# Three of eight experts in plain fp32 on 64 columns, two array halves, alternating with the others

## The chip, the cores and the metric

The kernel runs on one core of one Trainium2 chip. The metric is the device time of one execution in microseconds (us), the median of three runs. The five engines have queues of their own and meet at semaphores: TensorE (PE in the profile), VectorE (DVE), ScalarE (ACT), GpSimd (POOL) and SyncE (SP, which here issues the weight loads).

## The reference

A trunk of two layers on 256 tokens of width 1024, all in float32: retention and a dense SwiGLU in the first, a state-space mixer (S5) and a mixture of experts in the second, each behind a root-mean-square norm and added to the residual, and a last norm. What the change touches is the mixture: eight experts with a hidden width of 3584, of which each token uses two.

```python
logits = xf @ router
top_logits, top_idx = lax.top_k(logits, 2)
gates = softmax(top_logits)
# for each expert e, on the tokens that chose it:
y = (silu(x @ w_gate[e]) * (x @ w_up[e])) @ w_down[e]
# each token: the sum of its two experts' rows, times their gates
```

256 tokens with two choices are 512 rows, 64 an expert on average. Each expert has 44 MB of weights, 352 MB in all.

## The kernel before, in words

**Units.** All weights stream through SBUF in units of 1 MB, 128 partitions by 2048 numbers. SP loads unit n (L549 to L571) into one of six raw slots, and may do so when DVE has split the unit that held the slot (the wait at L569; the profile has the load itself at L570). ACT copies it, rounded, into one of three slots `weights_hi` (L892 to L901), as soon as it has landed and TensorE is done with the unit three before. DVE writes the rest, raw minus hi, into `weights_lo` (L1267 to L1271). TensorE then makes each product from three (L1751 to L1755): hi x hi, hi x lo, lo x hi, each at the rate of the rounded type. A unit is 12 matmuls of 128 stationary columns (the tokens) on 512 moving columns (the weights).

**Experts.** An expert has 42 units in 21 blocks of two (L1934 to L1968, `ffn`). The hidden width is cut in seven steps of 512, and the order is gate 0, up 0, then for s = 1 to 6 gate s, up s, down s-1, and down 6 at the end. ACT takes silu of the gate bank, DVE multiplies by the up bank (`act_rows`), TensorE transposes the four tiles of that (`turn`), and ACT and DVE split it, for the down units to use. ACT and DVE have this work written out between their splits, by the unit's number in the expert (L962 to L985, L1351 to L1378), and do it in that order. All eight experts use 128 slots of rows, in the order of their numbers. A second pass follows only if an expert has over 128 tokens; with these inputs it is skipped.

**Rows.** DVE picks the first expert's rows with a product against a pick matrix. POOL works out each row's slot in a chain of small operations, writes the normed rows to a table in HBM with four indirect DMAs (L841), then works out where they come back from. SP loads an expert's 128 rows of that table into `slot_rows` (L587) and TensorE turns them (L2252) ahead of the expert's last down block; SP also writes the result rows out (L591). The last expert's result doesn't go by HBM but by a product. POOL fetches the other rows back (L860) during the last expert.

Of the kernel before, what the change touches and what calls it, by code (L numbers as in the profile page):

```python
# [14 lines left out]
F32 = mybir.dt.float32  # L15
# [50 lines left out]
SPARE_U0 = MOE_U0 + RAW + AHEAD  # L66

# [99 lines left out]
def trunk(nc, A, consts, out):  # L167
    with ExitStack() as ctx:
# [84 lines left out]
        put_g = place("put_gated", [TT, P], F32, K_OFF + 26624)  # L253
        final_gain = place("final_gain_row", [D], F32, H_OFF + 16384)
# [9 lines left out]
        def small(name, shape, dt=F32):  # L264
            size = -(-4 * math.prod(shape) // 32) * 32
            small_at[0] += size
            assert small_at[0] <= H_OFF
            return place(name, shape, dt, small_at[0] - size)

# [37 lines left out]
        key = small("slot_key", [TT, EXPERTS])  # L307
        r_second = small("is_in_second_pass", [TT, EXPERTS])
# [47 lines left out]
        unused_set = sem("unused_set")  # L356
# [11 lines left out]
        warm_ready = sem("warm_rows_ready")  # L368
# [75 lines left out]
        counted = sem("tokens_counted")  # L444
# [95 lines left out]
        def _(sp):  # L540
# [8 lines left out]
            def load(n, kt, src, e=None):  # L549
# [5 lines left out]
                else:  # L555
                    signal = landed[ring_number(n, e) % RAW]
                    if n >= RAW:
# [11 lines left out]
                        sp.wait_ge(lo_ready, count(last + 1, e, FFN_UNITS))  # L569
# [11 lines left out]
            for p in range(2):  # L581
                sp.dma_start(from_slots[p][0:1, :], zeros[0:1, :]).then_inc((y_sent, nothing_landed)[p], 16)

            def slot_range(p, e):
                return bass.ds(e * SLOTS + (1 + ROWS * p), SLOTS)

            def load_slots(p, e):  # L587
                sp.wait_ge(gathered, count(EXPERTS * p, e, 1))
                sp.dma_start(slot_rows[:, :], to_slots[slot_range(p, e), :]).then_inc(slots_landed, 16)

            def send_y(p, e):  # L591
                sp.wait_ge(y0_copied, count(EXPERTS * p + 1, e, 1))
                sp.wait_ge(y1_copied, count(EXPERTS * p + 1, e, 1))
                sp.dma_start(from_slots[p][slot_range(0, e), :], y_rows[:, :]).then_inc(y_sent, 16)

            def experts(p):
                u0 = MOE_U0 + p * EXPERTS * FFN_UNITS
                if p:
                    load_slots(p, 0)

                def expert(e, first, last):
                    for i, (kt, src) in enumerate(ffn_sources(
                            A["moe_w_gate"][0, e], A["moe_w_up"][0, e], A["moe_w_down"][0, e])):
                        if i == 10 and not first:
                            send_y(p, e - 1)
                        if i == 24 and not last:
                            if first and not p:
                                sp.wait_ge(rows_sent, 16 * 2 * TT)
                            load_slots(p, e + 1)
                        load(u0 + i, kt, src, e)  # L610

                expert(0, True, False)
                with sp.Fori(1, LAST) as e:
                    expert(e, False, False)
                expert(LAST, False, True)

            experts(0)
            sp.wait_ge(keys_done, 1)
            flag = sp.value_load(over[0:1, 0:1], min_val=0, max_val=1)
            with sp.If(flag > 0):  # L620
                experts(1)
                send_y(1, LAST)
# [7 lines left out]
        def _(pool):  # L630
# [195 lines left out]
            tt(choice[1][:, :, :], chosen[:, :, :], choice[0][:, :, :], ALU.subtract)  # L826
            pool.wait_ge(pick_ready, 1)
            ts(r_second[:, :, :], key[:, :, :], float(SLOTS), None, ALU.is_gt, ALU.bypass)
            tt(r_cum[:, :, :], key[:, :, :], first_row, ALU.add)
            ts(row_of[0][:, :, :], r_second[:, :, :], float(ROWS - SLOTS), None, ALU.mult, ALU.bypass)  # L830
            tt(r_cum[:, :, :], r_cum[:, :, :], row_of[0][:, :, :], ALU.add)
# [6 lines left out]
            pool.wait_ge(nothing_landed, 16 * (2 * EXPERTS + 1))  # L838
            for t in range(TT):
                for j in range(2):  # L840
                    pool.indirect_dma_start(to_slots, bass.IndirectOffsetOnAxis(ap=pair_i[:, 0, j, t:t + 1], axis=0),  # L841
                                            hn[:, t, :], None).then_inc(rows_sent, 16)
            tt(row_of[1][:, :, :], r_cum[:, :, :], r_second[:, :, :], ALU.mult)
            tt(row_of[0][:, :, :], r_cum[:, :, :], row_of[1][:, :, :], ALU.subtract)
            link(nc.gpsimd.memset(row_of[0][:, :, LAST:EXPERTS], 0.0))
# [5 lines left out]
            both_choices(share[:, :, :], gate_w[:, :, :])  # L851
            nc.gpsimd.tensor_copy(pair_i[:, 1:3, :, :], pair[:, 1:3, :, :]).then_inc(shares_ready, 1)
# [11 lines left out]
            pool.wait_ge(y_sent, 16 + 16 * LAST)  # L864
# [3 lines left out]
            with pool.If(flag > 0):  # L868
                pool.wait_ge(y_sent, 16 + 16 * (LAST + EXPERTS))
                pool.wait_ge(scatter_added, 1)  # L870
                rows_come_back(1)
# [3 lines left out]
        def _(act):  # L875
# [16 lines left out]
            def split_hi(n, e=None):  # L892
# [6 lines left out]
                if n >= SPLIT:  # L899
                    act.wait_ge(used, count(n - SPLIT + 1, e, FFN_UNITS))  # L900
                copy(w_hi[:, n % SPLIT, :], raw_unit(n, e)).then_inc(hi_ready, 1)  # L901

            def norm_rows():

                act.wait_ge(unused_set, 1)
# [56 lines left out]
            def ffn(u0, s0, tts, e=None, each=None):  # L962

                silu_at = {ffn_first(s) + 4: s for s in range(STEPS)}
                evac_at = {7 if s == 0 else 41 if s == STEPS - 1 else 6 * s + 6: s for s in range(STEPS)}
                for i in range(FFN_UNITS):
                    if i in silu_at:
                        s = s0 + silu_at[i]

                        act.wait_ge(used, count(u0 + ffn_first(silu_at[i]) + 2, e, FFN_UNITS))  # L970
                        if s:
                            act.wait_ge(mult_done, count(s, e, STEPS))
                        nc.scalar.activation(gated[:, 0:tts, :], PS[:, 0:tts, :], ACT.Silu).then_inc(silu_done, 1)
                    if i in evac_at:
                        s = s0 + evac_at[i]
                        act.wait_ge(act_t_done, count(s + 1 - STEPS, e, STEPS))
                        copy(ht_hi[evac_at[i] % 2][:, 0:tts, :, :],
                             PS[:, tts:2 * tts, :].rearrange("p t (f c) -> p t f c", f=FT)).then_inc(act_hi, 1)
                    if each:
                        each(i)  # L980
                    if i < AHEAD:
                        continue
                    split_hi(u0 + i, e)

# [201 lines left out]

            def gather_hi(g):
# [4 lines left out]
            def y_out(p, e):  # L1192
                act.wait_ge(used, count(MOE_U0 + (p * EXPERTS + 1) * FFN_UNITS, e, FFN_UNITS))
                if not (isinstance(e, int) and e == 0 and p == 0):
                    act.wait_ge(y_sent, count(16 + 16 * (EXPERTS - 1) * p, e, 16))
                copy(y_rows[:, 0:512], PS[:, 4, :]).then_inc(y0_copied, 1)

            def last_y_out():

                act.wait_ge(first_half_done, 1)  # L1200
                act.wait_ge(y_sent, 16 + 16 * LAST)
                copy(y_rows[:, 0:512], PS[:, 4, :]).then_inc(y0_copied, 1)

            def experts(p):
                u0 = MOE_U0 + p * EXPERTS * FFN_UNITS
                if p:
                    gather_hi(EXPERTS * p + 1)
                    for i in range(AHEAD):
                        split_hi(u0 + i)

                def expert(e, first, last):
                    def each(i):
                        if i == 2 and not first:
                            y_out(p, e - 1)
                        if i == 19 and last and p == 0:
                            act.wait_ge(put_t_done, 1)
                            copy(put_g[:, :, :], PS[:, 6, 0:2 * P].rearrange("p (a b) -> p a b", a=2)).then_inc(put_ready, 1)
                    ffn(u0, STEPS * (1 + EXPERTS * p), 1, e, each)
                    if not last:
                        gather_hi(count(EXPERTS * p + 2, e, 1))  # L1220
                        for i in range(AHEAD):
                            split_hi(u0 + FFN_UNITS + i, e)
# [6 lines left out]
            experts(0)  # L1229
            act.wait_ge(keys_done, 1)  # L1230
            flag = act.value_load(over[0:1, 0:1], min_val=0, max_val=1)
            with act.If(flag > 0):
                last_y_out()
                experts(1)
                y_out(1, LAST)
# [19 lines left out]
        def _(dve):  # L1255
# [11 lines left out]
            def split_lo(n, e=None):  # L1267

                dve.wait_ge(hi_ready, count(n + 1, e, FFN_UNITS))
                tt(w_lo[:, n % SPLIT, :], raw_unit(n, e), w_hi[:, n % SPLIT, :].bitcast(F32),  # L1270
# [80 lines left out]
            def ffn(u0, s0, tts, e=None, each=None):  # L1351
                mult_at = {ffn_first(s) + 6: s for s in range(STEPS)}
                evac_at = {7 if s == 0 else 41 if s == STEPS - 1 else 6 * s + 6: s for s in range(STEPS)}
                for i in range(FFN_UNITS):
                    if i in mult_at:
                        s = s0 + mult_at[i]
                        dve.wait_ge(silu_done, count(s + 1, e, STEPS))

                        dve.wait_ge(used, count(u0 + ffn_first(mult_at[i]) + 4, e, FFN_UNITS))
# [980 lines left out]
```

## Time and profile before

| what | value |
|---|---|
| median of three runs | 1580.86 us (1580.41 to 1581.86) |
| span of the profiled execution | 1580.7 us, 23580 instructions |
| PE, PEld busy | 1565.6, 1306.7 us |
| DVE, ACT, POOL busy | 1213.7, 982.1, 271.8 us |
| HBM read, written | 461.23 MB, 15.21 MB, 301 GB/s over the span |

Busy times are of one profiled execution, whose own time is its span. A matmul's record is longer than its share of the engine's time, because matmuls overlap; the distance between the starts of two of them is what one costs. PEld is the load of stationary columns, beside the matmuls. A wait is put down to what ended it. The DMA share counts the time of packets, and can pass 1.

### The profile page before, as it was taken

To read this page: it belongs to the slowest core of one execution; us is meant where nothing else is said; L and a number is where in the kernel's file an instruction comes from. 1 tells how busy PE (TensorE), PEld (TensorE's weight loads), DVE (VectorE), ACT (ScalarE), POOL (GpSimd) and SP (SyncE) were. 2 spreads that over 40 slices of the span, in tenths; PEclk is the share of its full clock that TensorE was granted. 3 is DMA by queue.
4 is the path that set the end of the run, shared out by engine and by line. 5 is a ranking of instruction groups with operands and counts; after the bars stand their busy time and mean duration, and the time that the engine had idled before them with its cause. 6 is when DMAs were issued, how large, how long until landed. Compare 5 with 4: busy or idle time off the path is not lost.

```text
span 1580.7 us, 23580 instructions
## 1 busy us (share of the span) xinstructions
PE 1565.6 (99%) x9466; PEld 1306.7 (83%) x9466; DVE 1213.7 (77%) x825; ACT 982.1 (62%) x732; POOL 271.8 (17%) x244
## 2 busy tenths in 40 slices
PE   9999999999999999999999999999999999999997
PEld 8788889999988888888888888888888888888885
DVE  5556566555558658888888888888888888888897
ACT  5443454333454347777777777777777777777775
POOL 5599316200037008100000000000000000000100
PEclk9999999999999999999999999999999999999999
DMA  9544657865511368999999999999999999999993
GB/s 350 171 159 156 205 161 274 298 200 185 186 38 57 115 247 316 394 392 371 381 362 366 383 367 361 388 364 363 384 371 352 387 371 352 387 374 347 398 392 147
DMA packets 202143, 469.18 MB, mean 297 GB/s; under 512 B 7784, under 2 KB 20288, under 8 KB 202064
## 3 DMA queue, kind: packets, MB, share of 16 engines
q1 hardware_dynamic: 199872, 461.13, 80.7%
q0 software_dynamic: 2048, 6.88, 1.5%
q8 instruction: 55, 0.90, 0.2%
q14 instruction: 24, 0.20, 0.0%
q10 hardware_dynamic: 144, 0.07, 0.0%
HBM read 461.23 MB, written 15.21 MB: 301 GB/s over the span
## 4 chain that ended last, share of the span: by engine, by line
PE 93%; DVE 3%; ACT 2%; POOL 1%; issue 1%; DMA 0%; ACTq 0%; DVEq 0%; POOLq 0%
PE PS L1746 90%; PE PS L1875 2%; DVE weights_lo L1265 1%; ACT weights_hi L884 1%; POOL b_padded L784 1%; PE PS L2096 0%; ACT c_padded L884 0%; PE PS L2255 0%; DVE residual L1265 0%; POOL param_tmp L643 0%; DMA constants<-in_constants 0%; DVE act_rows L1265 0%; PE PS L1845 0%; ACT x_transposed_hi L934 0%; DVE act_rows L1416 0%
## 5 line engine op out<-in xcount | busy, mean ns | idle before, releaser
L1265 DVE TENSOR_TENSOR weights_lo<-weights_raw,weights_hi 128x2048 fp32r<-128x2048 f32 (+1 forms) x419 | 963.0, 2307 | 254.5 <-ACT weights_hi L884 252.9
L884 ACT ACTIVATE weights_hi<-weights_raw 128x2048 fp32r<-128x2048 f32 (+1 forms) x419 | 800.9, 1913 | 364.1 <-PE PS L1746 354.9
L1746 PE MATMUL PS<-weights_hi,gathered_hi 128*128 128x512 f32 x896 | 355.1, 396 | 0.3 <-DVE gathered_lo L1627 0.3
L1746 PE MATMUL PS<-weights_hi,gathered_lo 128*128 128x512 f32 x896 | 355.1, 396 | 0.0
L1746 PE MATMUL PS<-weights_lo,gathered_hi 128*128 128x512 f32 x896 | 352.3, 393 | 0.0
L1746 PE MATMUL PS<-weights_hi,act_transposed_hi 128*128 128x512 f32 x624 | 252.8, 405 | 0.0
L1746 PE MATMUL PS<-weights_hi,act_transposed_lo 128*128 128x512 f32 x624 | 247.1, 396 | 0.0
L1746 PE MATMUL PS<-weights_lo,act_transposed_hi 128*128 128x512 f32 x624 | 245.8, 394 | 0.0
L1746 PEld LDWEIGHTS PS<-weights_hi,gathered_lo 128*128 128x128 f32 x896 | 168.2, 188 | 41.2
L1746 PEld LDWEIGHTS PS<-weights_lo,gathered_hi 128*128 128x128 f32 x896 | 168.2, 188 | 41.1
L1746 PEld LDWEIGHTS PS<-weights_hi,gathered_hi 128*128 128x128 f32 x896 | 168.2, 188 | 40.0 <-DVE gathered_lo L1627 0.4
L1746 PE MATMUL PS<-x_transposed_hi,weights_hi 128*128 128x256 f32 x640 | 181.2, 283 | 1.3 <-DVE weights_lo L1265 1.1
L1746 PE MATMUL PS<-x_transposed_lo,weights_hi 128*128 128x256 f32 x640 | 179.7, 281 | 0.0
L1746 PE MATMUL PS<-x_transposed_hi,weights_lo 128*128 128x256 f32 x640 | 179.7, 281 | 0.0
L860 POOL DMA_INDIRECT row_back<-results_by_slot,pair_index x4 | 7.4, 1861 | 824.8 <-DMA results_by_slot<-expert_rows 823.9
L1746 PEld LDWEIGHTS PS<-weights_hi,act_transposed_lo 128*128 128x128 f32 x624 | 117.1, 188 | 28.6
L1746 PEld LDWEIGHTS PS<-weights_lo,act_transposed_hi 128*128 128x128 f32 x624 | 117.4, 188 | 26.5 <-issue 0.7
L1746 PEld LDWEIGHTS PS<-weights_hi,act_transposed_hi 128*128 128x128 f32 x624 | 117.3, 188 | 25.7 <-issue 0.7
L1746 PEld LDWEIGHTS PS<-x_transposed_hi,weights_hi 128*128 128x128 f32 x640 | 120.7, 189 | 2.6 <-DVE weights_lo L1265 1.3
L1746 PEld LDWEIGHTS PS<-x_transposed_lo,weights_hi 128*128 128x128 f32 x640 | 120.7, 189 | 0.3
L1746 PEld LDWEIGHTS PS<-x_transposed_hi,weights_lo 128*128 128x128 f32 x640 | 120.7, 189 | 0.0
L1746 PE MATMUL PS<-weights_hi,x_transposed_hi 128*128 128x512 f32 x192 | 76.2, 397 | 0.1
(283 smaller groups left out, 1273.4 us busy)
## 6 DMA issues: line engine op xcount, KB each, us to landing
weights_raw<-in_moe_w_up SPq DMA_DIRECT2D x111, 1024.0 KB, 6.8
weights_raw<-in_moe_w_down SPq DMA_DIRECT2D x111, 1024.0 KB, 6.6
weights_raw<-in_moe_w_gate SPq DMA_DIRECT2D x110, 1024.0 KB, 6.8
weights_raw<-in_ret_w_in SPq DMA_DIRECT2D x24, 1024.0 KB, 6.6
weights_raw<-in_ffn_w_gate SPq DMA_DIRECT2D x14, 1024.0 KB, 5.2
weights_raw<-in_ffn_w_up SPq DMA_DIRECT2D x14, 1024.0 KB, 5.1
weights_raw<-in_ffn_w_down SPq DMA_DIRECT2D x14, 1024.0 KB, 4.9
weights_raw<-in_ret_w_out SPq DMA_DIRECT2D x8, 1024.0 KB, 4.9
```

Source lines behind the costliest of these rows:

```text
L784: nc.gpsimd.tensor_scalar(b_pad[:, i0:i1, :, :, c].rearrange("p i j m n -> p (i j) m n"), rows.rearrange("p i j m n -> p (i j) m n"), cst[ ...
L860: pool.indirect_dma_start(back[t][j][:, :], None, from_slots[p], bass.IndirectOffsetOnAxis(ap=pair_i[:, 1 + p, j, t:t + 1], axis=0)).then_ ...
L884: return nc.scalar.activation(o, i, ACT.Copy)
L1265: return nc.vector.tensor_tensor(o, a, b, op)
L1746: return nc.tensor.matmul(o, l, r, start=start, stop=stop)
L1875: ins = nc.tensor.transpose(PS[:, bank, ft * P:(ft + 1) * P], act_rows[:, t, ft * P:(ft + 1) * P], ident)
```

## The change

The eight experts are put in a new order at run time. Expert 0 stays first. POOL sorts the others by their count of tokens, and ranks 1, 2 and 3, the three with the fewest, are the light ones; ranks 4 to 7 follow. SP reads each expert's number from SBUF and loads by it. The light ones have room for 64 rows each (an excess goes to the second pass). With the inputs used, experts 0 to 7 get 59, 61, 70, 66, 70, 59, 72 and 55 rows by the reference, so the light ones have 55, 59 and 61. Their units aren't split: TensorE reads the raw slot as the moving operand of plain fp32 products, with the 64 tokens as the stationary columns of one half of the array. In gate and up units one half takes the first 256 columns of the weights and the other half the last; in down units each half takes 512 of the 1024. So an unsplit unit's raw slot comes free when TensorE has used the unit. Split units have a count of their own for the `weights_hi` slots.

The order of units is: expert 0 whole; two blocks of rank 4; then a block of the heavy ranks and one of the light in turn, 63 times; then the last 19 blocks of rank 7. ACT's and DVE's small work for a light block stands at the second heavy unit two heavy blocks on. Slots are loaded and results sent by POOL, two halves of 512 columns for a light result, and the gathered rows are turned and copied in two halves through one bank in place of two.

Core of the diff:

```diff
+FIRST, LIGHT, HEAVY = 0, (1, 2, 3), (4, 5, 6, 7)
+BLOCKS = [("gate", 0), ("up", 0), *((kind, s - (kind == "down")) for s in range(1, STEPS) for kind in ("gate", "up", "down")),
+          ("down", STEPS - 1)]
+LAG = 2
+def small_after(k):
+    j = k - LAG
+    return j if 0 <= j < len(LIGHT) * len(BLOCKS) else None
+def units_in_order():
+    order = [(FIRST, i) for i in range(FFN_UNITS)]
+    for k in range(len(HEAVY) * len(BLOCKS)):
+        for ranks, at in ((HEAVY, k), (LIGHT, small_after(k))):
+            if at is not None:
+                q, b = block_of(ranks, at)
+                order += [(q, 2 * b), (q, 2 * b + 1)]
+    return order
...
@@ SP, load @@
-                        sp.wait_ge(lo_ready, count(last + 1, e, FFN_UNITS))
+                        if is_whole(last):
+                            sp.wait_ge(lo_ready, count(splits(last), e, FFN_UNITS))
+                        else:
+                            sp.wait_ge(used, last + 1)
...
@@ SP, order of the loads @@
+                for m, (q, i) in enumerate(ORDER):
+                    if q not in expert:
+                        if len(expert) == 1:
+                            sp.wait_ge(shares_ready, 1)
+                        expert[q] = sp.value_load(expert_at_i[0:1, q:q + 1], min_val=1, max_val=EXPERTS - 1)
...
@@ POOL, ahead of the rows' numbers (12 operations), more behind the scatters @@
+            pool.wait_ge(count_ready, 1)
+            ts(sort_key[:, :], token_count[:, :], float(EXPERTS * SLOTS), None, ALU.mult, ALU.bypass)
+            tt(sort_key[:, :], sort_key[:, :], expert_row, ALU.add)
...
+            tt(table[:, :, :], inner(sort_key[:, :]), outer(sort_key[:, :]), ALU.subtract)
+            ts(table[:, :, :], table[:, :, :], 0.0, None, ALU.is_lt, ALU.bypass)
+            over_table(rank[:, :])
...
@@ ACT, split_hi @@
-                    act.wait_ge(used, count(n - SPLIT + 1, e, FFN_UNITS))
+                    act.wait_ge(used, count(SPLIT_UNITS[SPLIT_NUMBER[n] - SPLIT] + 1, e, FFN_UNITS))
...
@@ DVE, behind split_lo(MOE_U0 + 2) @@
+            nc.vector.tensor_copy(token_count[:, :], PS[:, 6, 64:64 + EXPERTS]).then_inc(count_ready, 1)
...
@@ DVE, small work @@
+            def after_small(j):
+                q, b = block_of(LIGHT, j)
+                kind, s = BLOCKS[b]
+                if kind == "up":
+                    done = STEPS * (q - LIGHT[0]) + s
+                    dve.wait_ge(silu_small, done + 1)
+                    dve.wait_ge(used, NUMBER[q, 2 * b + 1] + 1)
+                    if done:
+                        dve.wait_ge(turned_small, done)
+                    tt(act_small[:, :], gated_small[:, :], PS[:, 2, 0:HALF_FC], ALU.mult).then_inc(mult_small, 1)
...
@@ DVE (and ACT likewise), for unit i of the heavy rank number at @@
+                        if at:
+                            l = FFN_UNITS * (at - 1) + i
+                            j = small_after((l - 5) // 2) if l % 2 else None
+                            if j is not None:
+                                after_small(j)
+                        if at or i >= AHEAD:
+                            split_lo(number(i))
...
@@ PE, a light block @@
+                def turn(s):
+                    pe.wait_ge(mult_small, STEPS * (q - LIGHT[0]) + s + 1)
+                    for i in range(2):
+                        ins = nc.tensor.transpose(PS[:, 2, i * P:(i + 1) * P], act_small[:, i * P:(i + 1) * P], ident)
+                    ins.then_inc(turned_small, 1)
+                if kind == "down":
+                    if s < STEPS - 1:
+                        turn(s + 1)
...
+                                ins = mm(PS[tile[dh], 7, :], act_t_small[s % 2][:, ft, :], w[:, k, dh * 512:dh * 512 + 512],
+                                         s == 0 and ft == 0, s == STEPS - 1 and ft == FT - 1)
...
+                if kind == "gate":
+                    if s == 1:
+                        turn(0)
...
+                        for h in range(2):
+                            ins = mm(PS[tile[h], bank, 0:HALF_FC], x_small[:, kt, :], w[:, k, h * HALF_FC:(h + 1) * HALF_FC],
+                                     kt == 0, kt == KT - 1)
```

## Rows read from the trace of the kernel before

**Rows 1.** The page: busy us of the engines; granted clock in 40 slices.

```profile
PE 1565.6 (99%) x9466; PEld 1306.7 (83%) x9466; DVE 1213.7 (77%) x825; ACT 982.1 (62%) x732; POOL 271.8 (17%) x244
...
PEclk9999999999999999999999999999999999999999
```

**Rows 2.** Who waited for whom, 640 to 1580 us: us in total, times, longest.

```profile
ACT weights_hi L884 <- PE PS L1746: 172.3, 233, 1.2
...
SPq L570 <- DVE weights_lo L1265: 727.8, 314, 3.7
```

**Rows 3.** Gathered rows' tile (count, ns, starts); the chain from 560 us.

```profile
L1746 PEld LDWEIGHTS PS<-weights_hi,gathered_hi x896: 186/188/191, 596.6 to 1556.3; 128*128 128x128 f32 x180
...
L884 ACT ACTIVATE gathered_hi<-PS x7: 1027/1035/1035, 713.3 to 1442.5; 128x1024 fp32r<-128x1024 f32 x7
...
623.35 16.80 PE PS L1746 x72
640.15 0.44 PE PS L1875 x4
```

**Rows 4.** Stretches: busy us by engine, clock, DMA share, GB/s; landing us.

```profile
620.00:700.00 80.00, 79.90 (x354) 64.22 (x353) 69.83 (x42) 57.94 (x37) 19.10 (x23) 1.00 1.04 396
...
730.00:1440.00 710.00, 710.00 (x3155) 573.47 (x3154) 615.22 (x340) 517.82 (x339) 0.00 (x0) 1.00 1.01 372
...
weights_raw<-in_moe_w_down SPq DMA_DIRECT2D x12, 1024.0 KB, 9.2
...
weights_raw<-in_moe_w_down SPq DMA_DIRECT2D x12, 1024.0 KB, 5.8
...
weights_raw<-in_ffn_w_down SPq DMA_DIRECT2D x14, 1024.0 KB, 4.9
```

**Rows 5.** In order of time: plain fp32 weight loads; quarter tiles, what follows.

```profile
50.77 0.19 PEld L1746 LDWEIGHTS PS<-v_rows,scores_transposed 128*128 128x128 f32 x1 [0.24 <-issue]
51.20 0.19 PEld L1746 LDWEIGHTS PS<-v_rows,scores_transposed 128*128 128x128 f32 x1 [0.24 <-issue]
...
493.61 2.00 PE L1746 MATMUL PS<-states,c_padded 128*32 128x64 f32 x128
495.54 0.38 PE L1746 MATMUL PS<-x_transposed_hi,weights_hi 128*128 128x256 f32 x1
495.76 0.28 PE L1746 MATMUL PS<-x_transposed_lo,weights_hi 128*128 128x256 f32 x1
495.88 0.28 PE L1746 MATMUL PS<-x_transposed_hi,weights_lo 128*128 128x256 f32 x1
```

**Rows 6.** Groups by form, 700 to 1500 us: split and small DVE operations.

```profile
L1265 DVE TENSOR_TENSOR weights_lo<-weights_raw,weights_hi 128x2048 fp32r<-128x2048 f32 x277 | 631.7, 2291 | 106.3 <-ACT weights_hi L884 106.0
L884 ACT ACTIVATE weights_hi<-weights_raw 128x2048 fp32r<-128x2048 f32 x276 | 528.9, 1917 | 148.5 <-PE PS L1746 144.7 <-DMA weights_raw<-in_moe_w_gate 1.6 <-DMA weights_raw<-in_moe_w_up 1.6
...
L1265 DVE TENSOR_TENSOR act_rows<-silu_of_gate,PS 128x512 f32<-128x512 f32 x46 | 31.3, 681 | 0.0
```

**Rows 7.** Stretches at the end, columns as in rows 4.

```profile
1572.00:1573.00 1.00, 0.43 (x2) 0.00 (x0) 0.83 (x2) 0.86 (x4) 0.00 (x0) 1.00 0.08 16
1576.00:1577.00 1.00, 0.00 (x0) 0.00 (x0) 0.00 (x1) 0.00 (x0) 0.00 (x0) 1.00 0.16 53
1577.00:1578.00 1.00, 0.00 (x0) 0.00 (x0) 0.00 (x0) 0.00 (x0) 0.00 (x0) 0.50 0.94 385
```

**Rows 8.** POOL, DVE and SP in order of time.

```profile
604.16 0.19 POOL L834 CAST pair_index<-pair 128x4 int32<-128x4 f32 x1
...
613.61 0.23 POOL L640 TENSOR_TENSOR row_of_pass<-count_of_second,is_in_second_pass 128x16 f32<-128x16 f32 x1
...
639.88 0.19 POOL L852 CAST pair_index<-pair 128x8 int32<-128x8 f32 x1
...
599.03 2.29 DVE L1265 TENSOR_TENSOR weights_lo<-weights_raw,weights_hi 128x2048 fp32r<-128x2048 f32 x1 [0.23 <-ACT weights_hi L884]
...
699.63 3.17 SPq L570 DMA_DIRECT2D weights_raw<-in_moe_w_gate  x2
```

More of the change, by code:

```diff
@@ L581, in _ @@
             for p in range(2):
[L582 to L601, printed above, removed]
+                sp.dma_start(from_slots[p][0:1, :], zeros[0:1, :]).then_inc(nothing_landed, 16)
+            for q in LIGHT:
+                unfilled = 1 + q * SLOTS + SMALL_SLOTS
+                sp.dma_start(from_slots[0][unfilled:unfilled + SLOTS - SMALL_SLOTS, :],
+                             zeros[0:SLOTS - SMALL_SLOTS, :]).then_inc(nothing_landed, 16)
@@ L602, in expert, with second_pass @@
+            def second_pass():
+                def expert(e):
                     for i, (kt, src) in enumerate(ffn_sources(
                             A["moe_w_gate"][0, e], A["moe_w_up"][0, e], A["moe_w_down"][0, e])):
[L604 to L617, printed above, removed]
+                        load(MOE_END + i, kt, src, e)
+                expert(0)
+                with sp.Fori(1, EXPERTS) as e:
+                    expert(e)
+            first_pass()
             sp.wait_ge(keys_done, 1)
@@ L1200, in last_y_out, with gather_small @@
                 act.wait_ge(first_half_done, 1)
-                act.wait_ge(y_sent, 16 + 16 * LAST)
+                act.wait_ge(y_sent, 16 * (len(WHOLE) - 1))
                 copy(y_rows[:, 0:512], PS[:, 4, :]).then_inc(y0_copied, 1)
[L1204 to L1215, printed above, removed]
+            def gather_small(q, half):
+                act.wait_ge(gathered, 2 * TURNS.index(q) + half)
+                rows, k = half_of_slots(half)
+                copy(x_small[:, k, :], rows[:, :, 0:SMALL_SLOTS]).then_inc(x_small_ready, 1)
@@ new lines, in first_pass, with second_pass, expert @@
+                        if at or i >= AHEAD:
+                            split_hi(number(i))
+            def second_pass():
+                gather_hi(2 * EXPERTS)
+                for i in range(AHEAD):
+                    split_hi(MOE_END + i)
+                def expert(e, first, last):
+                    for i in range(FFN_UNITS):
+                        expert_work(i, lambda i: MOE_END + i, STEPS * (1 + len(WHOLE)), e)
+                        if i == 2 and not first:
+                            y_out(MOE_END + FFN_UNITS, len(WHOLE) - 1, e - 1)
+                        if i >= AHEAD:
+                            split_hi(MOE_END + i, e)
@@ L1664, in add_back, with y_out @@
                                                     in1=resid[:, t, :], op0=ALU.mult, op1=ALU.add))
[L1666 to L1669 removed]
+            def y_out(done, n_sent, e=None):
+                dve.wait_ge(used, count(done, e, FFN_UNITS))
+                if n_sent is not None:
+                    dve.wait_ge(y_sent, count(16 * n_sent, e, 16))
@@ new lines, in second_pass, with turn_next @@
+            def second_pass():
+                turn_landed(16 * EXPERTS)
+                def expert(e, last):
+                    pe.wait_ge(xg_lo_ready, count(2 * len(WHOLE), e, 1))
+                    def turn_next(half):
+                        if half and not last:
+                            turn_landed(16 * EXPERTS + 16, e)
+                    for b in range(len(BLOCKS)):
+                        expert_block(b, lambda i: MOE_END + i, STEPS * (1 + len(WHOLE)), e, n_out=len(WHOLE), turn_next=turn_next)
```

595 lines of the change are left out of this document (403 added, 192 removed).

## The prediction

> **What bounds the kernel now.** The page comes first [rows 1]: TensorE is busy for 99% of a span of 1580.7 us. Its share alone says little, since its records overlap, so the waits of the expert stage come next [rows 2]: ACT waits for TensorE before it splits a unit, and SP waits 727.8 us for DVE to free a slot. Everything queues behind TensorE, and no load stands among the long waits. The stage itself: expert 0 begins at 596.6 us, and the gathered rows of the next experts are copied from 713.3 to 1442.5 us [rows 3], so six experts take 729.2 us, 121.5 each. That is 42 units of 1 MB; one lasts 2.80 us (72 matmuls in 16.80 us, 12 to a unit), with seven turns of 0.44 us [rows 3], and 0.8 us is left for the turning of the next rows.
>
> What a faster TensorE would meet is in the DMA rows [rows 4]. From 730 to 1440 us the queues moved 372 GB/s, which is only what TensorE consumed. From 620 to 700 us, refilling the ring, they moved 396 GB/s; down loads landed after 9.2 us (those issued from 616 to 700 us) in place of 5.8 (from 1000 to 1100): more waiting in the queue, hardly more rate. So 396 GB/s looks like a ceiling, and a unit costs 1.0486 MB / 396 = **2.65 us of DMA**, just under TensorE's 2.80. I read the change from here.
>
> **What a light unit costs.** The change takes 3 x 42 units out of the three-product form and computes each as eight plain fp32 products of 64 stationary columns, four on each half of the array. A plain fp32 product shows as two records, and on 512 columns their weight loads follow each other after 0.43 us [rows 5], 0.83 ns a column. The 64-column records on quarter arrays (128*32) would cost 53 ns each by that; 128 of them took 2.00 us, 14 ns apart, so 3.8 of four ran at once [rows 5]. Two halves should run 1.9 at once: 16 records x 256 columns x 0.83 ns / 1.9 = **1.8 us** in place of 2.80. The ends are 1.7 (two at once) and 3.4 (none). Changing the array's form: behind the quarter tiles the first full-width record starts 0.22 us before the second, where later ones are 0.12 apart [rows 5], so 0.1 us per change, six in twelve units. The Trainium skill, TensorEngine Tiling (Array Packing), Key Properties, says that changing the mode drains TensorE; the rows agree that it costs something, and little.
>
> **TensorE's new sum.** Twelve units, six heavy and six light, take 6 x 2.80 + 0.44 + 0.8 / 7 = 17.4, and 6 x 1.8 + 0.22 (a small turn is two transposes in place of four) + 0.6 = 11.6: 29.0 us. There are 252 mixed units, 21 such dozens: 609 us against 729.2. TensorE alone would save 120 us. The remaining 84 units of that kind of work (expert 0, four units, the last 38) stay as they are.
>
> **What is late next: the loads.** The same 252 units are 264.2 MB, and slots read (six of 0.52 MB) and results written (three of 0.52, three of 0.26) add 5.5 MB: at 396 GB/s 667 + 14 = 681 us. The gain falls to 48 us.
>
> **And a wait that the order makes.** Light units use the raw slot itself, so SP may refill it only when TensorE has finished the unit; heavy slots still come free at the split. Number the mixed units H0 H1 L2 L3 H4 H5 L6 L7 and so on; with six slots, H(n+6) is loaded when L(n) is done. DVE multiplies the small gate and up rows of a light "up" block in its turn with the second heavy unit two blocks on, hence behind the split of the first one. Say the up block is L6 L7: the multiply stands behind the split of H12. TensorE wants its result for the turn at the head of L10 L11, after H8 H9. H12's load is issued when L6 is done. So the chain is: load, 4.9 us, as in the dense layer, where the queue is half idle (the third landing row [rows 4]); ACT's half of the split 1.92; DVE's 2.29 [rows 6]; the multiply of 256 columns, not in the trace, between half and all of the 0.68 of 512 columns [rows 6], taken as 0.45; turn 0.22; light unit 1.8; 0.2 for five hand-overs. That is 4.9 + 6.9 = 11.8 us from one light unit's end to the next one's. Until then TensorE has L7, H8, H9: 7.6 us.
> DMA sees it so: four slots are refilled together at each pair of light units, 4 x 2.65 = 10.6 us of transfers, and the next refill comes after 11.8. The queue runs dry for **1.2 us** once per up block. In the other two cycles of three TensorE needs 29.0 / 3 = 9.7 us, less than 10.6, and the queue stays full. A light expert has 7 up blocks, so there are 21. What the two full cycles leave in the queue delays the chain's load, and the refills behind it alike, so the dozen is twelve transfers, its share of other traffic (14 / 21 = 0.7) and the dry time: 12 x 2.65 + 0.7 + 1.2 = 33.7 us. TensorE stands still for 33.7 - 29.0 = 4.7 of them, nearly all in one gap ahead of the turn. Sum: 667 + 14 + 21 x 1.2 = **706 us** against 729.2: minus 23.
> Bounds of the dry time: 0 if the refills overlap the chain, 2.3 if the load takes the 5.8 us of [rows 4] and the multiply 0.68: from minus 48 to nothing.
>
> **The clock.** A gap of 4.7 us is new for this kernel. TensorE's last matmul ends at 1572.4 us and the granted clock falls from 1.00 to 0.50, that is from 2.4 to 1.2 GHz, at 1577 us [rows 7], 4.6 us later; in all its earlier pauses, short ones, it stayed at full speed [rows 1]. Where it falls in a gap, the light unit behind the turn takes 1.8 us more, and that one lies in the chain; later units are covered by the full queue. Bounds: none, or 21 x 1.8 = 38 us. With one row to go by, and a gap barely over it, I take five gaps: plus 9.
>
> **The prologue.** Sorting experts by count is POOL's. The count reaches it behind DVE's split that starts at 599.0 and ends at 601.3 us; 30 small operations at 0.78 us (34 of them took from 613.6 to 640.1 [rows 8]) end at 625, the four scatters (604.2 to 613.6 us before) at 634, 48 more operations at 672. SP asks for the sorted numbers before the first load of the next expert, at 699.6 [rows 8]: 27 us of cover, so nothing. Were it gone, each late us would first eat the six filled slots. Two tiny matmuls more ahead of the ranks: 0.2 us on the path. POOL now issues slot loads and results (17 transfers); it has nothing else to do then, and SP's queue loses them. Each slot load is asked for two blocks ahead or more, 11 us, and is half a unit, which by the unit's 9.2 us of landing in a full queue [rows 4] is in time; a miss of a us or two would fall into the gaps.
> Heavy experts' turn into gathered rows goes in two halves; same work. The tail after the last matmul is unchanged.
>
> **Sum.** 1580.9 - 23 + 9 + 0.2 = 1567 us. The profiled span of 1580.7 is 0.2 below the median of the three runs, 1580.86, so the two may be exchanged; a measurement can tell some 0.2%, 3.2 us.
>
> **Rivals.**
> A, *DMA goes faster or never runs dry* (0.21). Then minus 48: 1533 us. For: the dry 1.2 us is a small difference of large numbers, and overlap would wipe it out. Against: 396 over 80 us with a long queue. The Trainium skill, DMA: Bandwidth & Descriptors, Measured, has 425 GB/s for a 16 MB load. By that figure a unit is 2.47 us and the sum 1527 or so, dry time grown to 1.9 us included; no row here holds it.
> B, *TensorE-bound* (0.03): 1461 us. It needs 270 MB in 609 us, 443 GB/s, which no row has.
> C, *the clock falls in nearly every gap* (0.22), **slower**. Place: the gap ahead of the small turn; price 1.8 us; it decides from 4.6 us of idle, and the sum passes the old time when 13 of 21 gaps are hit. All hit: 1558 + 38 = 1596 us. For: 4.7 is over 4.6. Against: one row, one fall.
> D, *the halves don't run at once* (0.03): 3.4 us a light unit, 38.6 us a dozen: +82, 1663. Against: the quarter tiles.
> E, *the queue is already full at 372 GB/s* (0.03), its busy share being 1.01 there against 1.04 [rows 4]: 725 + 25, 1602.
> F, *nothing comes of it* (0.02), because SP waits for the sort at the switch of experts long enough to eat the gain: near 1581. The other way not to do what it says, a light expert with over 64 rows and so a second pass, is excluded: the three have 55, 59 and 61.
> My forecast has 0.46, its own range 1555 to 1577. Faster by 0.2%: it, A and B, less its upper edge, 0.67; within 0.2%: that edge, F and C with half the gaps hit, 0.10; slower: C, D, E, 0.23. The range goes from A to the whole of C: 1530 to 1597.
>
> **What would show it.** Light matmuls in pairs, 16 records in 1.8 us. DMA near 395 GB/s in the mixed stretch, TensorE's busy share there near 85% with granted clock above 0.95. Waits of TensorE for DVE's small multiply, about 21, near 4.7 us each; that row is the heart of it. SP waiting for TensorE on light slots. POOL's last small operation near 672 us. I'm wrong if TensorE's waits end in splits or loads instead, if the mean clock is under 0.92, or if the mixed stretch moves over 405 GB/s.

## The result and the profile after

The changed kernel takes 1636.53 us (median of four runs, 1629.65 to 1637.60) against 1581.36 us of the kernel before on the same chip: a ratio of 1.0341 [1.0321, 1.0360]. That is 55 us slower, where 1567 us was predicted. One execution of the last kernel of the experiments took 2541.93 us at a mean granted clock of 0.555 and is left out of its time.

The page of the changed kernel: span, busy us of the engines, granted clock in 40 slices, and the shares of the engines in the chain that ended last.

```profile
span 1633.8 us, 22563 instructions
...
PE 1496.8 (92%) x9592; PEld 1139.5 (70%) x9592; DVE 907.4 (56%) x678; ACT 730.5 (45%) x613; POOL 317.2 (19%) x295
...
PEclk9999999999999999999988999899899989999999
...
PE 72%; DMA 14%; ACT 5%; issue 4%; DVE 3%; POOL 1%; SPq 0%; ACTq 0%; DVEq 0%; POOLq 0%
```

Against [rows 1], TensorE, DVE and ACT all have less to do (TensorE 69 us, DVE 306, ACT 252), and yet the span is 53 us longer. The first sign of the reason is the clock row: it was 9 throughout, and now it dips all along the mixed stretch (where heavy and light blocks alternate). The second is the list of waits, which comes next.

The waits of TensorE and of SP in the changed kernel, 740 to 1480 us (us in total, times, longest), then the row of that stretch with the columns of [rows 4].

```profile
PE PS L2253 <- DVE small_act_rows L1493: 96.2, 20, 6.3
PE PS L2011 <- DVE weights_lo L1493: 14.2, 14, 2.2
```

```profile
SPq L666 <- PE PS L2011: 554.5, 118, 13.4
SPq L666 <- DVE weights_lo L1493: 43.8, 32, 3.0
```

```profile
740.00:1480.00 740.00, 626.15 (x3197) 402.84 (x3197) 307.00 (x187) 264.48 (x214) 5.43 (x10) 0.92 0.92 344
```

The wait that the prediction called the heart of it is there: TensorE ahead of the small turn, for DVE's small multiply, 20 times in this stretch and once more outside it, 4.8 us each. But the DMA queues move 344 GB/s, less than the 372 of before [rows 4], although TensorE has less work. So the loads don't bound this stretch. Something keeps them from being asked for: SP waits 554 us for TensorE to give light slots back.

### The profile page after: what moved, and what is told of

The parts are those of the page before. It is cut to its first block, busy times and chain, and to the rows that moved or that the text cites. A ratio compares the mean times of both kernels' runs of the same rounds, so it can differ in the third digit from the quotient of the medians.

```text
span 1633.8 us, 22563 instructions
## 1 busy us (share of the span) xinstructions
PE 1496.8 (92%) x9592; PEld 1139.5 (70%) x9592; DVE 907.4 (56%) x678; ACT 730.5 (45%) x613; POOL 317.2 (19%) x295
## 4 chain that ended last, share of the span: by engine, by line
PE 72%; DMA 14%; ACT 5%; issue 4%; DVE 3%; POOL 1%; SPq 0%; ACTq 0%; DVEq 0%; POOLq 0%
PE PS L2011 69%; DMA weights_raw<-in_moe_w_down 8%; ACT weights_hi L1053 4%; DMA weights_raw<-in_moe_w_gate 3%; DMA weights_raw<-in_moe_w_up 2%; DVE weights_lo L1493 1%; PE PS L2140 1%; PE PS L2253 1%; DVE small_act_rows L1493 1%; PE PS L2581 1%; POOL b_padded L873 1%; PE PS L2412 0%; ACT c_padded L1053 0%; DVE residual L1493 0%; POOL param_tmp L732 0%
## 5 line engine op out<-in xcount | busy, mean ns | idle before, releaser
L1493 DVE TENSOR_TENSOR weights_lo<-weights_raw,weights_hi 128x2048 fp32r<-128x2048 f32 (+1 forms) x293 | 676.9, 2313 | 596.6 <-ACT weights_hi L1053 594.2
L1053 ACT ACTIVATE weights_hi<-weights_raw 128x2048 fp32r<-128x2048 f32 (+1 forms) x293 | 559.0, 1909 | 698.5 <-PE PS L2011 217.4
L2011 PE MATMUL PS<-weights_hi,gathered_hi 128*128 128x512 f32 x560 | 226.8, 405 | 11.4 <-DVE weights_lo L1493 10.7
L2011 PE MATMUL PS<-weights_hi,gathered_lo 128*128 128x512 f32 x560 | 222.4, 397 | 0.0
L2011 PE MATMUL PS<-weights_lo,gathered_hi 128*128 128x512 f32 x560 | 221.5, 396 | 0.0
L2011 PE MATMUL PS<-weights_hi,act_transposed_lo 128*128 128x512 f32 x456 | 180.3, 395 | 0.0
L2011 PE MATMUL PS<-weights_lo,act_transposed_hi 128*128 128x512 f32 x456 | 179.9, 394 | 0.0
L2011 PE MATMUL PS<-weights_raw,small_gathered 128*64 128x256 f32 x1344 | 160.7, 394 | 2.3 <-ACT small_gathered L1053 2.3
L2011 PEld LDWEIGHTS PS<-weights_raw,small_gathered 128*64 128x64 f32 x1344 | 95.6, 141 | 63.7 <-issue 19.6
L2011 PE MATMUL PS<-weights_raw,small_act_transposed 128*64 128x512 f32 x336 | 107.6, 799 | 0.0
```

The costliest lines, as they stand in the source:

```text
L1053: return nc.scalar.activation(o, i, ACT.Copy)
L1493: return nc.vector.tensor_tensor(o, a, b, op)
L2011: return nc.tensor.matmul(o, l, r, start=start, stop=stop)
```

## One gap, closely

Stretches of 1 us around one gap of the changed kernel, same columns (TensorE's busy time is the first, then the granted clock, DMA share and GB/s are the last three), and TensorE in order of time, the first light block of all and the one behind this gap.

```profile
1015.00:1016.00 1.00, 0.00 (x0) 0.00 (x0) 0.00 (x0) 1.00 (x1) 0.00 (x0) 1.00 1.04 381
1016.00:1017.00 1.00, 0.00 (x0) 0.00 (x0) 0.67 (x1) 0.30 (x1) 0.00 (x0) 0.90 1.06 391
1017.00:1018.00 1.00, 0.00 (x0) 0.00 (x0) 1.00 (x1) 0.90 (x1) 0.00 (x0) 0.50 1.06 389
...
1020.00:1021.00 1.00, 1.00 (x8) 0.51 (x6) 1.00 (x1) 0.00 (x0) 0.00 (x0) 0.50 0.92 336
1021.00:1022.00 1.00, 1.00 (x8) 0.62 (x6) 0.94 (x2) 0.00 (x0) 0.00 (x0) 0.50 0.26 92
1022.00:1023.00 1.00, 1.00 (x8) 0.54 (x6) 0.00 (x0) 0.00 (x0) 0.00 (x0) 0.50 0.00 0
1023.00:1024.00 1.00, 1.00 (x8) 0.57 (x6) 0.00 (x0) 0.00 (x0) 0.00 (x0) 0.69 0.00 0
1024.00:1025.00 1.00, 1.00 (x12) 0.56 (x8) 0.00 (x0) 0.00 (x0) 0.00 (x0) 1.00 0.52 45
```

```profile
735.21 3.67 PE L2011 MATMUL PS<-weights_raw,small_gathered 128*64 128x256 f32 x32
...
1019.01 0.69 PE L2253 MATMUL PS<-constants,small_act_rows 128*128 128x128 f32 x2 [4.39 <-DVE small_act_rows L1493]
1019.63 5.62 PE L2011 MATMUL PS<-weights_raw,small_gathered 128*64 128x256 f32 x32
```

TensorE's last matmul ends at 1014.6 us. The clock falls to 0.50 (1.2 GHz) at 1016.8, 2.2 us later, and is back at about 1023.6 (0.69 on the average of that us). The pause is over at 1019.0, so the turn and nearly the whole light block behind it run at half speed: 5.62 us for two light units, where the first such block, with a warm clock, takes 3.67. The queue meanwhile has nothing left at 1021.3 and is idle until 1024, because the slots that it could refill are those of this light block.

Read in the same way in quarters of a us, **all 21 gaps** of the kernel bring the clock down, 2.2 to 4.8 us after the last matmul's end, and it stays low for 3.3 to 10.3 us, 115 us in all. Where it falls late, TensorE is already at work again.

The chain through another gap (start us, us, what).

```profile
1069.68 7.54 DMA weights_raw<-in_moe_w_down
...
1077.25 1.92 ACT weights_hi L1053
...
1079.25 2.14 issue
1081.39 0.43 DVE small_act_rows L1493
...
1081.87 0.69 PE PS L2253 x2
1082.56 3.15 PE PS L2011 x8
...
1085.86 7.89 DMA weights_raw<-in_moe_w_gate
```

It has the members that were predicted, in their order (the 2.14 us of issue are DVE's split, which goes on): load, half split, other half, multiply, turn, light unit, next load. But it is 16.2 us from load to load and not 11.8. The load lands after 7.5 us in place of 4.9, the turn takes 0.69 in place of 0.22, and the light unit 3.15 in place of 1.8.

## The experiments

Theory K: the small multiply in DVE's order makes a chain that leaves the queues dry once per up block, and the low clock in the same gap lengthens it. Rivals: the queues are slower for a reason of their own, TensorE's own work sets the pace, or the gap costs little and the clock everything. Every kernel below was timed beside the kernel before (1581.5 to 1581.6 us). Line numbers of the edits are those of the changed kernel.

### 1 and 2: the small work earlier

The chain exists only because DVE multiplies behind the split of the first heavy unit of a block (odd l). In the first kernel DVE does so one unit earlier (the edit stands at L1947); in the second ACT does its part earlier too (the same edit at L1428).

```
-    j = small_after((l - 5) // 2) if l % 2 else None
+    j = small_after((l - 4) // 2) if l % 2 == 0 else None
```

> Only DVE's small multiply moves, from behind the split of the first heavy unit two blocks on to ahead of it. Theory (the gap of 4.8 us in each dozen of units is the wait for that multiply, and the clock that falls in it costs 1.8 us more): the 21 waits of the small turn shrink from 101 us to under 10, the mean granted clock of the mixed stretch rises from 0.93 to above 0.98, and a dozen units takes what the loads take, 12 x 2.68 + 0.7 = 32.9 us in place of 36.7. 21 x 3.8 = 80 us less, about 1556 us. Rival (345 GB/s is all that the loads reach when light units hold their raw slots): the wait moves to the splits and the time stays above 1620 us.

> As the run before, with ACT's small work (silu, the copies of the turned and gathered rows) moved one unit ahead as well. Theory: only the stalls at the switch of light experts are left to gain, some 1 to 2 us at two places and less elsewhere, so 0 to 6 us faster than the run before. Rival (ACT's work ahead of the split delays the heavy units' split): slower than the run before by 21 times some 0.4 us, 8 us.

Measured: 1546.76 us, ratio 0.9776 [0.9760, 0.9793], and 1539.08 us, ratio 0.9730 [0.9713, 0.9746]. One DVE instruction moved ahead by one unit is worth 90 us, moving ACT's with it 8 more (80 and up to 6 had been expected). The mixed stretch of the kernel with the multiply alone moved, then its waits of TensorE there; behind them the same of the kernel with both moved:

```profile
740.00:1480.00 740.00, 676.96 (x3538) 454.25 (x3535) 365.30 (x221) 312.99 (x249) 16.43 (x17) 0.97 1.03 387
```

```profile
PE PS L2011 <- DVE weights_lo L1493: 40.8, 41, 2.7
PE PS L2011 <- ACT small_act_transposed L1053: 11.6, 4, 4.1
PE PS L2581 <- ACT small_gathered L1053: 5.8, 2, 2.9
```

```profile
740.00:1480.00 740.00, 677.66 (x3584) 458.61 (x3584) 375.73 (x227) 322.17 (x254) 15.73 (x17) 0.99 1.04 394
```

```profile
PE PS L2011 <- DVE weights_lo L1493: 55.1, 55, 2.1
```

The wait for the small multiply is gone from both. What ACT did late shows in the first as waits of two kinds, up to 4.1 and 2.9 us long, and is gone in the second. In the second the queues move 394 GB/s without a pause, and TensorE waits for split units, at most 2.1 us at a time: the stretch is bound by the loads, as experiment 4 confirms. It beats both kernels, and comes near what rival A described (1533 us).

### 3: the gap kept, its standstill filled

Ahead of the small turn TensorE does 16 products of the identity that nobody reads, so it doesn't stand still; the chain is untouched.

```
 def turn(s):
+    pe.wait_ge(silu_small, STEPS * (q - LIGHT[0]) + s + 1)
+    for _ in range(16):
+        mm(PS[:, 6, 2 * P:3 * P], ident, ident, True, True)
     pe.wait_ge(mult_small, STEPS * (q - LIGHT[0]) + s + 1)
```

> The changed kernel with 16 transposable 128-column fp32 products of the identity put ahead of each small turn (3.4 us of work nobody reads), so that TensorE pauses for little over 1 us. All waits stay. Theory of the clock: it stays at 1.00, the turn takes 0.25 in place of 0.69 us and the light unit behind it 1.7 in place of 3.15, 1.9 us for each of 21 chains: 40 us less, about 1596 us. Rival (the clock's fall is hidden, since the loads bound the time): within 5 us of 1636.

Measured: 1605.26 us, ratio 1.0148 [1.0131, 1.0165]. The clock is worth 31 us (40 were expected), and without its help the chain alone keeps the kernel 24 us slower than before. Of the filled kernel: the chain through one gap, the waits for the multiply, and stretches of 1 us behind that gap.

```profile
1057.66 8.15 DMA weights_raw<-in_moe_w_down
...
1065.84 1.92 ACT weights_hi L1053
...
1067.85 2.15 issue
1069.99 0.42 DVE small_act_rows L1493
...
1070.46 0.44 PE PS L2256 x2
```

```profile
PE PS L2256 <- DVE small_act_rows L1493: 26.8, 20, 2.7
```

```profile
1071.00:1072.00 1.00, 1.00 (x6) 0.31 (x6) 1.00 (x1) 0.00 (x0) 0.00 (x0) 1.00 1.04 381
1072.00:1073.00 1.00, 1.00 (x6) 0.29 (x4) 1.00 (x2) 0.00 (x0) 0.00 (x0) 1.00 0.54 201
1073.00:1074.00 1.00, 1.00 (x8) 0.29 (x4) 0.47 (x1) 0.00 (x0) 0.00 (x0) 1.00 0.09 23
1074.00:1075.00 1.00, 1.00 (x7) 0.50 (x4) 0.00 (x0) 0.00 (x0) 0.00 (x0) 1.00 0.91 117
1075.00:1076.00 1.00, 1.00 (x6) 0.82 (x5) 0.00 (x0) 0.00 (x0) 0.00 (x0) 1.00 1.03 385
```

SP issues the next load at 1072.94 us, as its row in order of time has it:

```profile
1072.94 2.09 SPq L666 DMA_DIRECT2D weights_raw<-in_moe_w_gate  x2
```

The queue had begun to run out half a us before, and is at its full rate only at 1075, two us behind the issue. Adding what each row falls short of 390 GB/s gives 0.5 + 0.9 + 0.7 = 2.1 us, in this gap: about 0.5 ahead of the issue and 1.6 behind it. The same in stretches of 4 us, the first up to this issue and the second from it:

```profile
1068.94:1072.94 4.00, 2.80 (x15) 1.11 (x16) 3.83 (x4) 1.60 (x1) 0.00 (x0) 1.00 0.94 345
1072.94:1076.94 4.00, 4.00 (x19) 2.35 (x16) 0.53 (x1) 0.00 (x0) 0.00 (x0) 1.00 0.75 225
```

Against 394 GB/s (the rate of the second kernel) the first lost 0.5 us and the second 1.7. Over all 21 gaps the stretches ahead of the issue lost 1.0 us each, from 0.1 to 3.2, and those behind it 1.7 each, never under 1.5. So most of the loss is the start of a load into a queue that has run out, and it comes in every gap. With smaller dips elsewhere the account below gives 3.2 us per gap, in place of the predicted 1.2. The Trainium skill, "SBUF — State Buffer", section "The DMA setup-cost knee", says that a transfer pays about 2 us that don't depend on its size, and puts most of that at its end. The size agrees with the two us here, the place doesn't: here they lie between the issue and the full rate.

### 4: half of the light products left out

The second kernel, with half of the products of each light unit left out (half of the sum over the rows of each weight unit isn't computed).

> The second kernel with half of each light unit's products left out (its output is not the reference's): TensorE has 23.9 us of work in a dozen units in place of 29.0, all loads stay. Theory (with the multiply early, the loads bound the mixed stretch): within 6 us of the second kernel, and DMA at 385 to 400 GB/s in the stretch. Rival (TensorE's work or the release of the raw slots still bounds it): faster than the second kernel by more than 15 us.

Measured: 1537.26 us, ratio 0.9717 [0.9701, 0.9734], 394 GB/s, TensorE busy for 600 of the 740 us in place of 678. It had 78 us less to do there and the time moved by 2: with the early multiply the loads are the bound, and a faster light unit would bring nothing. Its row, then its longest wait of TensorE:

```profile
740.00:1480.00 740.00, 600.18 (x2759) 421.88 (x2758) 376.45 (x227) 322.30 (x253) 15.72 (x17) 0.95 1.04 394
```

```profile
PE PS L2011 <- DVE weights_lo L1493: 129.5, 62, 3.7
```

The granted clock is lower here than in the second kernel, 0.95 against 0.99, because it falls in some of TensorE's many waits for a split. The time didn't suffer: with the loads as the bound, the low clock cost nothing here.

### 5: the same on the filled kernel

> The kernel with filled gaps, with half the products of each light unit left out (half of the sum over the rows of each weight unit is not computed). The filled kernel stands at 1605.3 us: dozens of 34.9 us, of which the queue spends 2.9 dry. Theory K: the dozen is twelve transfers plus the dry time, and the dry time is the chain from one light unit's end to the next one's (load, split, multiply, turn, light unit) less the four transfers. The chain holds just one light unit, which gets shorter by 0.85 us; the other work that TensorE saves (5 x 0.85 us a dozen) is given back as longer gaps. So 21 x 0.85 = 18 us less: about 1587 us, DMA share 0.98 to 0.99 in the mixed stretch, and the gap behind the filling longer. The longer gap may bring the low clock back; then only the turn and one half light unit are hit (0.2 + 0.85 us), and the time lies between 1587 and 1610. Theory T (TensorE's own sum sets the dozen): 21 x 6 x 0.85 = 107 us less, bounded by the loads at 1539. Theory R (the dozen is set by a lower rate of the queue, 358 GB/s, for another reason): no change, 1605 us with the same gaps.

Measured: 1574.45 us, ratio 0.9958 [0.9944, 0.9971], 31 us less than the filled kernel where 18 were expected from the chain. Theories T (1539) and R (1605) are out. K had the direction, but was 13 us short. One row of its chain hints at why:

```profile
1076.46 10.62 DMA weights_raw<-in_moe_w_down
```

A load took 10.6 us there. The likely reason is that TensorE, done earlier with the other light units, gives their slots back sooner, so that more stands in the queue when the gap comes. In some gaps it doesn't run dry: around the issue at 1059.54 us it moves 387 GB/s in the 4 us before and 306 in the 4 us after, where the filled kernel had 345 and 225 above. The waits for the multiply went from 20 to 11. So the other work in the dozen isn't all given back, as K had it. The mean clock is 0.95 here too (row below, 0.99 in the filled kernel), and it falls mostly in waits for splits; what that costs was not measured.

### 6 and 7: half the filling, and a longer chain

Two more versions of the filled kernel. In one, range(16) becomes range(8). In the other the multiply is done three times over, with range(20):

```
+for _ in range(2):
+    link(tt(act_small[:, :], gated_small[:, :], PS[:, 2, 0:HALF_FC], ALU.mult))
 tt(act_small[:, :], gated_small[:, :], PS[:, 2, 0:HALF_FC], ALU.mult).then_inc(mult_small, 1)
```

> The filled kernel with 8 unused products in place of 16 ahead of the small turn, so the pause behind them is about 1.2 + 1.9 = 3.1 us in place of 1.2 (4.8 in the changed kernel). In the changed kernel the clock fell in all 21 gaps, 2.3 to 4.8 us after the last matmul's end; in 8 of the 21 it was low by 3.0 us. Theory W (the fall comes at a time of its own, and what decides is how much of the pause lies before it): the clock falls in some 8 to 12 of the 21 pauses, the time is 1605 + 8 to 12 times 1.5 = 1617 to 1623 us, mean clock near 0.98. Theory L (it falls after 4.6 us of standstill, as at the end of the kernel before): it falls in none, 1605 us. Theory S (any pause of over 2 us brings it down): in nearly all, close to 1636 us.

> The filled kernel with the small multiply done three times, one behind the other (the same values are written), and 20 unused products in place of 16 so that TensorE's pause stays near 1.3 us. Theory K (the dozen is twelve transfers plus the dry time, set by the chain): the chain grows by 2 x 0.42 us and two hand-overs of about 0.05, 0.9 us; the dry time and with it the dozen grow by the same, in 21 dozens 19 us: about 1624 us. DVE is busy for little over half of the span, so a theory by which the time is set anywhere else (the rate of the queue, TensorE's sum) expects no change: 1605 us.

Measured: 1620.81 us for half the filling and 1621.75 us for the multiply thrice; the ratio of each is 1.0245 [1.0225, 1.0266]. The second is near what K asks for (1624), and no other theory asks for a change: 0.9 us on DVE, which is busy for little over half of the span, cost 16.5 us, so a us on the chain counts 18 times, nearly the 21 of the count of gaps.

For half the filling the time is that of theory W, but not for its reason. The clock fell in 19 of the 21 pauses, as theory S had it, and not in 8 to 12. Only it stayed low for less (79 us in all against 115 in the changed kernel), and often from a moment at which TensorE was already at work again. So the number of falls was wrong by a factor of two and the cost of each as well: 15.6 us over 19 falls, 0.8 us each, against 31 / 21 = 1.5 in the changed kernel.

### All of them in one account

If the dry time is what all this is about, then the transfers lost in these 740 us of the mixed stretch must give the time. With the loads always busy the kernel takes 1539.1 us at 394 GB/s. A kernel that moves x GB/s over the same 740 us has lost 740 (1 - x / 394) us:

| kernel | GB/s | lost, us | time above 1539.1, us |
|---|---|---|---|
| multiply early | 387 | 13 | 7.7 |
| filled, half products | 373 | 39 | 35.4 |
| filled | 358 | 68 | 66.2 |
| filled by half | 351 | 81 | 81.7 |
| filled, multiply thrice | 350 | 83 | 82.7 |
| changed kernel | 344 | 94 | 97.4 |

The rows from which the middle column comes, of the filled kernel, of half the filling, of the multiply thrice and of half the products:

```profile
740.00:1480.00 740.00, 689.55 (x3985) 484.94 (x3980) 320.70 (x195) 276.69 (x222) 5.98 (x11) 0.99 0.96 358
```

```profile
740.00:1480.00 740.00, 665.15 (x3579) 446.33 (x3579) 313.97 (x192) 270.39 (x218) 5.98 (x11) 0.95 0.94 351
```

```profile
740.00:1480.00 740.00, 693.38 (x4077) 495.71 (x4075) 329.01 (x231) 268.33 (x216) 5.97 (x11) 0.99 0.94 350
```

```profile
740.00:1480.00 740.00, 634.57 (x3268) 464.99 (x3266) 341.72 (x209) 294.01 (x235) 16.95 (x17) 0.95 0.99 373
```

The two columns agree within 6 us for six kernels, so nothing of size is hidden outside the mixed stretch. The columns don't say where in it the transfers are lost. The stretches of 4 us do, ahead of the first issue behind each of the 21 turns and behind it, read as in experiment 3 (sums of 21, in us):

| kernel | lost ahead of the issue | lost behind it |
|---|---|---|
| filled | 22 | 36 |
| filled, multiply thrice | 41 | 36 |
| filled by half | 42 | 36 |
| changed kernel | 56 | 37 |

A longer chain and a low clock add to the first column. The multiply done thrice adds 19 us there, which is its 0.9 us 21 times. The second column, the start of the load, is the same in all four.

## Why the prediction was wrong

It was wrong in sign. The members of its chain and their order were right, and rival C (0.22) names the smaller part of what was missing; the larger part, the start of a load into an empty queue, stood in no term and in no rival. Its signs came out but for two that matter: the mixed stretch ran at 344 GB/s and not near 395, and its mean clock was 0.92 and not above 0.95.

- **What bounds the kernel, and the loads as the next bound: right.** With the chain removed the kernel stands at 1539.1 us, 42 us below before, where 48 were worked out from 396 GB/s. The queues did 394 (3.5 of the 6 us). Over this stretch no kernel reached 405 GB/s, nor the 425 of the Trainium skill (DMA: Bandwidth & Descriptors, Measured).
- **The light unit: right.** Two of them take 3.67 us here, where 3.6 was worked out; the halves of the array do run at once. The small multiply took 0.42 to 0.43 us, where 0.45 was taken. The small turn's record was 0.44 us with a warm clock, where 0.22 was taken.
- **"The queue runs dry for 1.2 us": the first step that failed.** It was 68 / 21 = 3.2 us with a warm clock, 66 us in the sum instead of 25, and above the upper bound of 2.3. With the 394 GB/s it turns minus 23 into plus 24, a kernel slower than before. The step set the 11.8 us of the chain against 10.6 us of transfers, as if a refill moved at full rate from its issue. What it meant by dry, the queue run out ahead of the issue, was 1.0 us per gap, close to its 1.2. But behind the issue another 1.7 us was lost in each gap until the load was under way, 36 us in all, and that was put at nothing. The chain was longer too, 15.3 us from issue to issue (1057.66 to 1072.94), mostly because its load landed after 8.15 us and not 4.9. The bound of 5.8 us for the landing came from a stretch in which a load is asked for every 2.8 us, one at a time. Here the queue still holds the refills of the two cycles before, and the four loads behind a turn are issued within 3 us. This did little harm: the queue was moving meanwhile, as the step had argued of the backlog. How the longer landing divides between the backlog and sharing was not measured.
- **"I take five gaps" for the clock: the second.** All 21 were hit. The price of 1.8 us was close: 31 / 21 = 1.5 on average. It added 31 us where 9 stood; the whole of rival C's 38 was nearer. The length of the gap came out too, 4.8 against 4.7 us, in part by luck: 4.7 was worked out from a dozen of 33.7 us, and the dozen took 36.7 (20 dozens from the turn at 758.64 to that at 1492.64 us). But the point from which it decides was read from one fall, 4.6 us after the last matmul [rows 7]. In the changed kernel it fell as early as 2.2 us after. The Trainium skill, "TensorE: Matmul & The Clock Gate", section "HAM oscillation — how this bites in real kernels", tells of a kernel whose waits between short bursts bring the clock down every time round; the 21 of 21 agree with it, and the prediction should have weighed it. The pauses of experiment 4 didn't all bring it down.
- **The range** ended at rival C with the dry time of the forecast (1597). The two bounds belong together, since the gap is the place of both: 38 us of clock and a dry time at its upper bound, 23 more, would have given about 1620, still short of 1636.5.
- **The prologue: nothing, as said.** POOL's last small operation starts at 683.45 us, 12 later than estimated, and its first slot load at 684.64. SP's first load of a sorted expert is issued at 697.97 us, against 699.6 before [rows 8].

POOL and SP in order of time in the changed kernel:

```profile
683.45 0.19 POOL L978 CAST pair_index<-pair 128x8 int32<-128x8 f32 x1
```

```profile
697.97 3.16 SPq L666 DMA_DIRECT2D weights_raw<-in_moe_w_gate  x2
```

Sum, with what the runs gave: 1581 - 42 (loads at 394 GB/s, never dry) + 66 (dry time) + 31 (clock) = 1636 us. It closes by construction, since each term is the difference of two of these kernels. What bears out the name dry time is the account of the transfers above.

## What to carry to other kernels

When a unit of work stops passing through a split and uses the load's own slot, its slot comes free later, and every instruction between its operands and its end now stands in the load's loop: walk the order of each engine from "slot free" to "slot free", and move a small instruction ahead of any large one that waits for a later load (here one DVE instruction, 90 us). Cost such a loop from the first byte of one load to the first byte of the next with the queue as full as it will be, and where the queue runs out, add the start of the next load (1.7 us lost here, every time). A new pause of TensorE of a few us that recurs is to be priced with the clock down every time, if the work behind it lies in that loop; where it doesn't, as in experiment 4, the low clock cost nothing.

## What was not expected of the hardware

- The granted clock doesn't fall a fixed time after the last matmul. In the changed kernel it was between 2.2 and 4.8 us, and in the kernel with half the filling it fell in every pause of 2.97 us or more, often after TensorE had started again. Over the three filled kernels with whole products, of the pauses ahead of the small turn between 1.8 and 2.75 us seven brought it down (the shortest 1.82 and 1.88) and two of 2.7 us didn't, and those of 0.8 to 1.7 us never did.
- The length of the pause alone doesn't decide it. In experiment 4 six pauses of 3.1 to 3.2 us passed at full clock, and five others of that length brought it down. One that passed, and the stretch around it (clock 1.00):

```profile
899.20 0.48 PE L2011 MATMUL PS<-weights_hi,gathered_hi 128*128 128x512 f32 x1 [3.11 <-DVE weights_lo L1493]
```

```profile
896.00:906.00 10.00, 6.89 (x32) 5.04 (x32) 4.91 (x3) 3.95 (x4) 0.00 (x0) 1.00 1.03 407
```

- Keeping TensorE at work with products that nobody reads was worth 31 us, 2% of the kernel, though it shortened nothing.
